# A transformer on one core: the first gate tile behind two feed-forward norms multiplies the stream before it is normalised

## The reference

```
def _rmsnorm(x, g):
    xf = x.astype(jnp.float32)
    y = xf * lax.rsqrt(jnp.mean(xf * xf, axis=-1, keepdims=True) + NORM_EPS)
    return (y * g.astype(jnp.float32)).astype(x.dtype)
...
        x = x + g1 * y
        h = _rmsnorm(x, norm2_g[i]) * (1.0 + sc2) + sh2
        x = x + g2 * _swiglu(h, ffn_w_gate[i], ffn_w_up[i], ffn_w_down[i])
...
def _swiglu(h, w_gate, w_up, w_down):
    return (jax.nn.silu(h @ w_gate) * (h @ w_up)) @ w_down
```

## Time and profile before

| | us |
|---|---|
| median of 3 runs | 1704.09 (1703.03 to 1704.3) |
| profiled execution, its own time | 1702.5 |
| its span | 1700.7 |
| TensorE busy | 1672.5 (98%) |
| VectorE busy | 1022.5 (60%) |
| ScalarE busy | 711.0 (42%) |
| GpSimd busy | 93.0 (5%) |
| TensorE's share of the chain that ended last | 91% |

### The profile page before, as it was taken

How to read it: one execution, slowest core, us unless ns; L and a number is a source line. 1 busy time by engine, 2 the same in 40 slices (tenths; PEclk the granted TensorE clock), 3 DMA queues, 4 the chain that set the end, 5 groups by cost and what they waited for, 6 DMA issues and landing times.

```text
span 1700.7 us, 23299 instructions
## 1 busy us (share of the span) xinstructions
PE 1672.5 (98%) x7872; PEld 1332.3 (78%) x7872; DVE 1022.5 (60%) x2002; ACT 711.0 (42%) x1344; POOL 93.0 (5%) x74
## 2 busy tenths in 40 slices
PE   9999999999999998999999999999999999999999
PEld 7687777778877776577888888887888788888887
DVE  8689786666667698846555653566454533333334
ACT  6666676653343336844233323234223433322322
POOL 2310000000000182100000000000000000000000
PEclk9999999999999999999999999999999999999999
DMA  5243444445531120012555553452323233333233
GB/s 209 75 150 100 150 153 154 151 158 193 189 112 57 56 75 26 1 53 72 201 194 198 198 198 99 131 178 87 99 87 99 86 92 95 99 99 94 93 100 109
DMA packets 56775, 202.82 MB, mean 119 GB/s; under 512 B 6576, under 2 KB 6704, under 8 KB 56560
## 3 DMA queue, kind: packets, MB, share of 16 engines
q1 hardware_dynamic: 56688, 201.68, 36.0%
HBM read 198.38 MB, written 2.10 MB: 118 GB/s over the span
## 4 chain that ended last, share of the span: by engine, by line
PE 91%; DVE 4%; ACT 2%; issue 1%; POOL 0%; DMA 0%; SPq 0%; DVEq 0%; ACTq 0%; POOLq 0%
PE bank L491 27%; PE bank L493 26%; PE bank L492 26%; PE bank L657 2%; PE bank L678 2%; PE bank L619 1%; PE bank L534 1%; PE bank L535 1%; PE bank L812 1%; PE bank L831 1%; DVE SB L2199 1%; ACT SB L1165 1%; PE bank L537 1%; PE bank L549 1%; PE bank L540 0%
## 5 line engine op out<-in xcount | busy, mean ns | idle before, releaser
L491 PE MATMUL bank<-H_hi,W_hi 128*128 128x512 f32 x1320 | 527.4, 400 | 3.3 <-DVE W_lo L1567 2.3
L492 PE MATMUL bank<-H_lo,W_hi 128*128 128x512 f32 x1320 | 514.4, 390 | 0.0
L493 PE MATMUL bank<-H_hi,W_lo 128*128 128x512 f32 x1320 | 514.3, 390 | 0.0
L1567 DVE TENSOR_TENSOR W_lo<-RAW,W_hi 128x512 fp32r<-128x512 f32 x526 | 345.9, 696 | 173.6 <-ACT W_hi L1006 157.8
L1006 ACT ACTIVATE W_hi<-RAW 128x512 fp32r<-128x512 f32 x538 | 317.6, 625 | 269.0 <-PE bank L493 236.3
L491 PEld LDWEIGHTS bank<-H_hi,W_hi 128*128 128x128 f32 x1320 | 247.7, 188 | 71.9 <-issue 18.1
L492 PEld LDWEIGHTS bank<-H_lo,W_hi 128*128 128x128 f32 x1320 | 247.9, 188 | 54.2 <-issue 4.8
L493 PEld LDWEIGHTS bank<-H_hi,W_lo 128*128 128x128 f32 x1320 | 247.8, 188 | 52.7
L493 PE MATMUL bank<-A_hi,W_lo 128*128 128x512 f32 x352 | 136.9, 389 | 0.0
L492 PE MATMUL bank<-A_lo,W_hi 128*128 128x512 f32 x352 | 136.9, 389 | 0.0
L491 PE MATMUL bank<-A_hi,W_hi 128*128 128x512 f32 x352 | 136.9, 389 | 0.0
(11 more groups left out here) (291 smaller groups left out, 2089.4 us busy)
## 6 DMA issues: line engine op xcount, KB each, us to landing
RAW<-weights SPq DMA_DIRECT2D x269, 512.0 KB, 3.7
AW<-ada SPq DMA_DIRECT2D x100, 512.0 KB, 3.7
X<-x_t SPq DMA_DIRECT2D x4, 512.0 KB, 7.6
y_t<-X SPq DMA_DIRECT2D x8, 256.0 KB, 2.0
LW<-lru_w SPq DMA_DIRECT2D x1, 1024.0 KB, 7.8
QX<-QR SPq DMA_DIRECT2D x40, 16.0 KB
...
```

Of the source, the lines that this page charges most:

```text
L491: pe.matmul(dst, wh, ch(hi, k), start=(k == 0), stop=False)
L492: pe.matmul(dst, wh, ch(lo, k), start=False, stop=False)
L493: mm = pe.matmul(dst, wl, ch(hi, k), start=False, stop=(k == chunks - 1))
L1567: dve.tensor_tensor(W_lo[:, w], RAW[:, c:c + HALF], W_hi[:, w], ALU.subtract).then_inc(lo_done, 1)
```

## The change

In both feed-forward norms, tile gate 0 no longer belongs to the pair. TensorE starts it right behind the residual's last tile, on unnormalised X * gain, split by ScalarE (MG_hi) and VectorE (MG_lo) while the residual stage runs. Its 24 matmuls take the place of the fill, with the sums and the row transposes between them. Sixteen matmuls of two columns multiply the same weights by the shift (SH, high and low part) into bank 6. At eviction VectorE multiplies bank 5 by rows (copied by ScalarE to SS) and ScalarE's Silu adds the shift's product as bias (RB).

The pair is now up 0 and gate 1; up 1 is the one single tile before the loop. The low halves of gate 1 and up 1 are made by GpSimd. ScalarE splits their high halves between the H_hi of the norm. The pieces left out of the diff are semaphores, arguments and the same calls for layer 1.

```diff
         COL = at("COL", 96)
+        put_hi, put_lo = (None, MG_hi, MG_hi), (None, MG_lo, YR_lo)
+        SH = at("SH", 16, None, F32R)
+        RB = at("RB", 4)
         SM = at("SM", 64)
...
-            def linear_pair(t0, idx, bank=PAIR_BANK):
+            def linear_pair(t0, idx, bank=PAIR_BANK, own=True):
...
                 if b.uses:
-                    pe.wait_ge(bank_free[b.bank], b.uses)
+                    pe.wait_ge(bank_free[b.bank], b.uses if own else b.uses - 1)
                 for k in range(KC):
...
                 return lambda k: square_sums(z, (SS,), False) if k == 5 else None
+            def put_off_chunk(tile, r, k):
+                if k % 4 == 0:
+                    pe.wait_ge(lo_done, tile.n * 2 + k // 4 + 1)
+                c = ((2 * tile.slot + k // 4) % 4) * HALF + (k % 4) * P
+                wh, wl = W_hi[:, c:c + P], W_lo[:, c:c + P]
+                pe.wait_ge(raw_hi_done, 8 * r + k + 1)
+                pe.matmul(ps[5][:], wh, ch(put_hi[r], k), start=(k == 0), stop=False)
+                pe.matmul(ps[5][:], wl, ch(put_hi[r], k), start=False, stop=False)
+                pe.matmul(ps[6][:, 0:2], wh, SH[:, 2 * k:2 * k + 2], start=(k == 0), stop=False)
+                mm = pe.matmul(ps[6][:, 0:2], wl, SH[:, 2 * k:2 * k + 2], start=False, stop=(k == KC - 1))
+                if k == KC - 1:
+                    mm.then_inc(shift_mm, 1)
+                pe.wait_ge(raw_lo_done, 8 * r + k + 1)
+                mm = pe.matmul(ps[5][:], wh, ch(put_lo[r], k), start=False, stop=(k == KC - 1))
+                if k % 4 == 3:
+                    mm.then_inc(used, 1)
+            def put_off(z, tile, r):
+                pe.wait_ge(shift_cols, r)
+                for k in range(3):
+                    put_off_chunk(tile, r, k)
+                square_sums(z, (ch(SQ, 1),), True)
+                for k in range(3, 6):
+                    put_off_chunk(tile, r, k)
+                pe.wait_ge(rinv_done, z + 1)
+                stat_rows((z % 2) * 24 + 16, 2).then_inc(stat_mm, 1)
+                for k in range(6, KC):
+                    put_off_chunk(tile, r, k)
...
                        between=early_sums(3) if q == 7 else None)
-            norm_stat(3, Tile(T_FFN0))
+            put_off(3, Tile(T_FFN0), 1)
...
                                between=early_sums(s) if q == 3 and s is not None else None)
-                if pair is not None:
+                if pair in (2, 4):
+                    linear_pair(t0 + 1, pair, own=False)
+                    linear(Tile(t0 + 3), hi, lo, own=False)
+                elif pair is not None:
                     linear_pair(t0, pair)
...
-            def norm_hi(idx, shift=None, third=None):
+            def norm_hi(idx, shift=None, third=None, raw=None):
                 for k in range(KC):
+                    if raw is not None and k == 0:
+                        split_hi(Tile(raw + 2), (0,), ACT.Identity)
+                    if raw is not None and k == 1:
+                        split_hi(Tile(raw + 2), (1,), ACT.Identity)
+                    if raw is not None and k == 6:
+                        split_hi(Tile(raw + 3), (0,), ACT.Identity)
                     if k == 7 and third is not None:
...
-            def pair_body(t0, i, fn, p0, dst_hi, b0, behind_norm=False):
+            def pair_body(t0, i, fn, p0, dst_hi, b0, behind_norm=False, raw=0):
...
                     first = behind_norm and q == 0
-                    if first:
+                    if first and raw:
+                        split_hi(Tile(t0 + 3), (1,))
+                    elif first:
                         split_hi(gb.next(), (1,))
...
                     act.wait_ge(prod_done, pn - 1)
-                    act.activation(ch(G1, par), ps[PAIR_BANK if first else ga.bank][:], fn).then_inc(fn_done, 1)
+                    if first and raw:
+                        act.wait_ge(raw_out, raw)
+                        act.activation(ch(G1, par), ch(Y2, 1 - par), fn, bias=RB[:, 2:3]).then_inc(fn_done, 1)
+                    else:
+                        act.activation(ch(G1, par), ps[PAIR_BANK if first else ga.bank][:], fn).then_inc(fn_done, 1)
                     act.wait_ge(fn_done, i * 2 + (b0 + q + 1))
                     act.sem_inc(bank_free[ga.bank], 1)
-                    split_hi(gb.next().next() if first else gb.next())
+                    if not (first and raw):
+                        split_hi(gb.next().next() if first else gb.next())
                     if dst_hi is not None:
...
-            def residual_squares(t0, c0):
+            def residual_squares(t0, c0, gain=None, r=0):
                 for k in range(KC):
...
                     square(k, c0 + k)
-            residual_squares(T_AO2, 24)
+                    if gain is not None:
+                        act.activation(ch(put_hi[r], k), ch(X, k), ACT.Copy, scale=gain(k)).then_inc(raw_hi_done, 1)
+            residual_squares(T_AO2, 24, lambda k: gcol(0, 1, k), 1)
             root(3, 1)
-            norm_hi(2, lambda k: mod(0, 3, k), Tile(T_FFN0 + 2))
+            norm_hi(2, lambda k: mod(0, 3, k), None, T_FFN0)
+            act.copy(SS[:, :], ps[2][:]).then_inc(rows_out, 1)
...
                         if kind[1] == 0:
-                            pair_body(t0, 0, ACT.Silu, pn, A_hi[0], pn, True)
+                            pair_body(t0, 0, ACT.Silu, pn, A_hi[0], pn, True, 1)
                         with act.Fori(1 if kind[1] == 0 else 0, bodies) as i:
...
                 pool.tensor_tensor(y_region(YA2_lo, s), heads, y_region(YA_hi, s), ALU.subtract).then_inc(y_lo_done, 1)
+            for t0 in (T_FFN0, T_FFN1):
+                pool.wait_ge(lo_done, 2 * (t0 + 2))
+                for t in (t0 + 2, t0 + 3):
+                    for half in range(2):
+                        low_half(Tile(t), half)
...
-            def residual(t0, c0, layer, m, x0):
+            def put_off_shift(layer, m):
+                cols = MOD[:, 48 * layer + 8 * m:48 * layer + 8 * m + 8]
+                sh = SH[:, :].rearrange("p (k two) -> p two k", two=2)
+                link(dve.tensor_copy(sh[:, 0], cols))
+                dve.tensor_tensor(sh[:, 1], cols, sh[:, 0], ALU.subtract).then_inc(shift_cols, 1)
+            def put_off_rms(z, t0):
+                variance(z, 1)
+                inverse(z, 1)
+                split_lo(Tile(t0 + 1), (1,))
+                dve.wait_ge(stat_mm, STAT_ROWS(z))
+            def put_off_out(t0, r):
+                dve.wait_ge(shift_mm, r)
+                link(dve.tensor_copy(RB[:, 0:2], ps[6][:, 0:2]))
+                link(dve.tensor_tensor(RB[:, 2:3], RB[:, 0:1], RB[:, 1:2], ALU.add))
+                dve.wait_ge(rows_out, r + 1)
+                ready(Tile(t0))
+                dve.tensor_tensor(ch(Y2, 1), ps[5][:], SS[:, :], ALU.mult).then_inc(raw_out, 1)
+            def residual(t0, c0, layer, m, x0, r=0, gain=None):
+                def low(k):
+                    dve.wait_ge(raw_hi_done, 8 * r + k + 1)
+                    dve.scalar_tensor_tensor(out=ch(put_lo[r], k), in0=ch(X, k), scalar=gain(k), in1=ch(put_hi[r], k),
+                                             op0=ALU.mult, op1=ALU.subtract).then_inc(raw_lo_done, 1)
...
                         split_lo(Tile(t0 + 9), (0,))
+                    if gain is not None and k:
+                        low(k - 1)
                     ready(tile)
...
                         sum_square(c0 + k, k == 0)
+                    elif gain is not None:
+                        low(7)
                     else:
...
-            residual(T_AO2, 24, 0, 2, 0)
-            inv_rms(3)
-            norm_lo(2, lambda k: gcol(0, 1, k), lambda k: mod(0, 3, k), Tile(T_FFN0 + 2))
+            put_off_shift(0, 3)
+            residual(T_AO2, 24, 0, 2, 0, 1, lambda k: gcol(0, 1, k))
+            put_off_rms(3, T_FFN0)
+            norm_lo(2, lambda k: gcol(0, 1, k), lambda k: mod(0, 3, k))
+            put_off_out(T_FFN0, 1)
...
                     tile = Tile(t0 + q, i)
+                    if behind_norm and q == 3:
+                        dve.wait_ge(lo_done, 2 * (t0 + 4))
                     if not behind_norm or q == 3:
                         split_lo(tile.next())
-                    elif q == 0:
-                        split_lo(Tile(t0 + 2), (1,))
                     if q % 2:
...
                         dve.wait_ge(a_lo_done, i * 2 + (y0 + h))
-                        dve.tensor_tensor(ch(Y2, par), ps[tile.bank][:], ch(G1, par), ALU.mult).then_inc(prod_done, 1)
-                        if behind_norm and q == 1:
-                            split_lo(Tile(t0 + 3))
+                        gated = ps[PAIR_BANK if behind_norm and q == 1 else tile.bank]
+                        dve.tensor_tensor(ch(Y2, par), gated[:], ch(G1, par), ALU.mult).then_inc(prod_done, 1)
                         dve.wait_ge(a_hi_done, i * 2 + (y0 + h + 1))
```

21 lines of the change are left out of this document (13 added, 8 removed).

## The result

| | before | changed |
|---|---|---|
| median of 20 runs each | 1703.88 us (1702.62 to 1705.13) | 1706.53 us (1704.58 to 1708.26) |
| ratio | | 1.0015, 95% interval 1.0009 to 1.0021 |
| profiled execution, own time | 1702.5 | 1707.18 |
| its span | 1700.7 | 1704.9 |

The changed kernel takes 2.65 us more.

What follows compares the result with a forecast made beforehand. TensorE, busy 98%, bounds the kernel. After 1.3 us contention per norm and late weights, the fifth tile loses 0.35 us in layer 0 and gains 1.3 in layer 1: 0.9 us faster, 1703.2, range 1699.0 to 1706.6.

Steps and rivals of the forecast that it cites:

- the put-off tile: Gate tile 0 in each feed-forward norm, replacing fill: pair starts 2.1 us later with 5.44 us done, 3.3 us gained per norm.
- The upper bound of 0.23 us for a small matmul: The sixteen two-column shift matmuls per norm: expected 0.10 us each, at most 0.23 us, as long as a wide one.
- the new chain: Work behind the pair's end, from VectorE's product and ScalarE's Silu to the fifth tile's W_lo, predicted late for TensorE.
- The stall at the fifth tile: TensorE's wait for VectorE's W_lo behind the pair and single tile: 2.4 us in layer 0, 0.7 us in layer 1.
- contention: GpSimd's low halves delay VectorE's H_lo in the pair: 1.3 us together, from 0 to 2.2; no contention had chance 0.14.
- the tie at tile four: Tile four's first low half on GpSimd, ready just as VectorE's H_lo is due: 0.4 to 1.0 us.
- the clock fall: Rival: layer 0's 2.4 us idle lowers TensorE's clock for 3.4 us, costing 1.7 us; 1704.9 in all, chance 0.14.
- a page's rule: The Trainium skill's clock rule, speaking of idle gaps: by it a stall inside dense work costs nothing more.
- the first G: VectorE's first operation for the pair in a norm, forecast at 789.9, 0.68 us behind the start of the row transposes.
- the chain behind E: E is the pair's end, forecast 804.2; behind it the fifth tile starts at E + 7.8 in layer 0, E + 6.15 in layer 1.
- dear small matmuls: Rival: shift matmuls at 0.23 us each cost 3.8 us, giving 1707.0; chance 0.10 together with all upper ends.
- the clock rival: Slower case: the granted clock drops behind layer 0's stall, 0.8 us slower with the sum, 1704.9; chance 0.14.

## Why the prediction was wrong, point by point

- **Right: the put-off tile.** Pair start 0.16 us off, a chunk 0.92 for 0.89, a small matmul 0.11 for 0.10, no idle ahead of the pair. The upper bound of 0.23 us for a small matmul is ruled out.
- **Right: the new chain.** The stall at the fifth tile was 2.31 and 0.68 us for 2.4 and 0.7; nothing behind it was late. The runs with earlier splits show that the order of splits and modulation steps is its cause.
- **Right mechanism, wrong size: contention.** "I take 1.3 us together, from 0 to 2.2": it was 1.8, since both meetings cost over half a microsecond and the tie at tile four most of a GpSimd operation (1.83 - 0.75 = 1.08 us). That is 0.5 us a norm, 1.0 in all, and eats the 0.9 us of gain. Taking GpSimd away moved the kernel by 2.2 us by the trace and 2.8 by the medians.
- **The failed step: the granted clock.** The prediction gave "the clock fall" 0.14 as a rival, priced it at 1.7 us, and left it out of the sum. The fall came, behind the stall of layer 0, and cost 1.70 us; the run with fill matmuls, which left the stall as it was, took it away. The evidence was in the prediction's own words: it forecast 2.4 us idle in one piece, and the earlier trace rows had a fall behind a microsecond in which TensorE was busy 0.14. I weighed that against a page's rule instead of taking the row. The Trainium skill (TensorE: Matmul & The Clock Gate, HAM oscillation) tells of falls behind gaps longer than this one; here 2.31 us were enough, and the measurement decides. The rival's mechanism, price and place were right; what failed is that the sum left it out.
- **The sum.** Forecast -0.9. Contention adds 1.0; the first G 0.1 later and the chain behind E 0.12 and 0.14 longer add 0.4 over both norms; the clock adds 1.7. That makes the trace's +2.2. The medians' further 0.4 us is no TensorE time: the time outside the span is longer by 0.85 us in the changed kernel by its median, and the spans' medians differ by 2.1; the prediction had no term for it.
- **Luck.** That 1706.53 lies just inside the range, which ends at 1706.6, is luck. The upper end took in dear small matmuls, which the trace rules out; the clock rival alone gave 1704.9.

The lag ahead of the edited part goes with the clock falls there: it is 0.59 to 0.98 us in the four changed kernels without a fall near 507 us and 1.32 to 2.77 in the seven with one. That none of the eleven is below 0.59 stays open; the profiled execution of the kernel before was itself 1.4 us under the median of its runs.
